# A hybrid conv / RG-LRU / mixture-of-experts step on one core: expert matmuls without high/low splits, the first chunk's matmuls reordered, token ranks dealt over gather rows

## The reference, cut to what matters

```python
def layer(x, cond, h0, on_grid, p):
    mod = (jax.nn.silu(cond) @ p['w_ada'] + p['b_ada'])[:, None, :]
    sh1, sc1, g1, sh2, sc2, g2 = jnp.split(mod, 6, axis=-1)
    h = rmsnorm(x, p['g_norm1']) * (1 + sc1) + sh1
    mix, h_last = token_mixer(h, h0, on_grid, p)     # u = h @ w_in (1024 x 7168), gates, two scans, w_o
    x = x + g1 * mix
    h = rmsnorm(x, p['g_norm2']) * (1 + sc2) + sh2
    return x + g2 * hier_moe(h, p), h_last

def hier_moe(h, p):
    ...   # group by argmax of 4 logits, then the top 2 of that group's 8 experts, weights in gates
    y = jnp.zeros_like(t)
    for e in range(N_EXPERTS):                        # 32; w1, w3: 1024 x 512, w2: 512 x 1024
        z = jax.nn.silu(t @ p['w1'][e]) * (t @ p['w3'][e])
        y = y + gates[:, e:e + 1] * (z @ p['w2'][e])
    return y.reshape(bsz, n, d)
```

## Time and profile before

| | |
|---|---|
| median of 3 runs | 1034.56 us (1031.83 to 1035.78) |
| the profiled execution | 1033.22 us |
| its span | 1031.5 us |
| PE busy (matmuls) | 937.8 us, 91% |
| DVE, ACT, POOL busy | 700.5, 569.7, 285.0 us |
| DMA packets | 69162, 294.97 MB, mean 286 GB/s |
| chain that ended last | PE 75%, DVE 13%, ACT 4%, DMA 2% |

### The profile page before, as it was taken

How to read it: one execution, slowest core, us unless ns; L and a number is a source line. 1 busy time by engine, 2 the same in 40 slices (tenths; PEclk the granted TensorE clock), 3 DMA queues, 4 the chain that set the end, 5 groups by cost and what they waited for, 6 DMA issues and landing times.

```text
span 1031.5 us, 12627 instructions
## 1 busy us (share of the span) xinstructions
PE 937.8 (91%) x4226; PEld 684.4 (66%) x4226; DVE 700.5 (68%) x881; ACT 569.7 (55%) x791; POOL 285.0 (28%) x214
## 2 busy tenths in 40 slices
PE   4499899998999999994899999999999999999980
PEld 2289797888999999444655656656656656566540
DVE  2389696859104442456788888887887888888835
ACT  4366536472334431311777677777767776776723
POOL 0235263635455553301011112112111211121010
PEclk9699899999999999995899999999999999999995
DMA  9992263646462656247589999999999999999804
GB/s 346 304 352 89 82 236 104 232 164 244 165 236 91 223 153 238 102 144 268 180 347 418 410 405 411 409 401 410 402 412 413 400 418 404 411 422 416 370 24 184
DMA packets 69162, 294.97 MB, mean 286 GB/s; under 512 B 8548, under 2 KB 19076, under 8 KB 56836
## 3 DMA queue, kind: packets, MB, share of 16 engines
q1 hardware_dynamic: 62740, 284.40, 71.5%
q0 software_dynamic: 5120, 6.31, 1.9%
q10 hardware_dynamic: 1264, 3.76, 1.0%
HBM read 290.20 MB, written 14.72 MB: 296 GB/s over the span
## 4 chain that ended last, share of the span: by engine, by line
PE 75%; DVE 13%; ACT 4%; issue 3%; SPq 3%; DMA 2%; POOL 0%; POOLq 0%; DVEq 0%; ACTq 0%
PE bank L936 21%; PE bank L919 13%; PE bank L920 12%; PE bank L796 7%; PE bank L798 6%; PE bank L797 6%; PE bank L845 3%; PE bank L909 2%; SPq L520 2%; DVE xcy L1504 2%; DVE lru L1558 1%; SPq L553 1%; ACT lru L1123 1%; DVE cp L1587 1%; DVE cp L1584 1%
## 5 line engine op out<-in xcount | busy, mean ns | idle before, releaser
L457 POOL TENSOR_TENSOR subs<-ring,subs 128x1024 fp32r<-128x1024 f32 x72 | 183.9, 2561 | 217.6 <-ACT subs L1046 217.6
L936 PE MATMUL bank<-ring,zT_buf 128*128 128x512 f32 x496 | 219.2, 595 | 0.0
L796 PE MATMUL bank<-h_hl,subs 128*128 128x384 f32 x512 | 177.7, 347 | 23.3 <-DVE h_hl L1482 14.7
L797 PE MATMUL bank<-h_hl,subs 128*128 128x384 f32 x512 | 175.0, 342 | 0.0
L798 PE MATMUL bank<-h_hl,subs 128*128 128x384 f32 x512 | 174.7, 341 | 0.0
L919 PE MATMUL bank<-subs,x_stack 128*128 128x512 f32 x384 | 162.5, 423 | 3.0 <-ACT x_stack L1310 1.7
L936 PEld LDWEIGHTS bank<-ring,zT_buf 128*128 128x128 f32 x496 | 91.9, 190 | 103.9 <-issue 103.8
L920 PE MATMUL bank<-subs,x_stack 128*128 128x512 f32 x384 | 154.1, 401 | 0.0
L513 DVE TENSOR_TENSOR subs<-ring,subs 128x1024 fp32r<-128x1024 f32 x96 | 112.2, 1222 | 25.5 <-ACT subs L1294 25.5
L796 PEld LDWEIGHTS bank<-h_hl,subs 128*128 128x128 f32 x512 | 98.0, 191 | 32.2 <-issue 18.2
L1046 ACT ACTIVATE subs<-ring 128x1024 fp32r<-128x1024 f32 x72 | 75.8, 1059 | 74.0 <-PE bank L798 66.6
(11 more groups left out here) (220 smaller groups left out, 1461.0 us busy)
## 6 DMA issues: line engine op xcount, KB each, us to landing
ring<-in_w SPq DMA_DIRECT2D x64, 2048.0 KB, 12.4
slot<-in_w SPq DMA_DIRECT2D x16, 2048.0 KB, 16.8
gate_w<-in_w SPq DMA_DIRECT2D x16, 2048.0 KB, 17.1
ring<-in_w_in SPq DMA_DIRECT2D x14, 2048.0 KB, 8.1
ring<-in_w_ada SPq DMA_DIRECT2D x12, 2048.0 KB, 20.0
ring<-in_w_rnn_out SPq DMA_DIRECT2D x2, 2048.0 KB, 7.8
ring<-in_w_conv_out SPq DMA_DIRECT2D x2, 2048.0 KB
ring<-in_w_o SPq DMA_DIRECT2D x2, 2048.0 KB, 7.9
```

Source lines behind the costliest of these rows:

```text
L457: eng.tensor_tensor(pair[:, 1], src, pair[:, 0].bitcast(F32), ALU.subtract).then_inc(done, 1)
L796: eng.matmul(ps[:, 0:T], pair[:, 1, k, :], x[:, 0, k, :], start=(k == 0), stop=False)
L797: eng.matmul(ps[:, 0:T], pair[:, 0, k, :], x[:, 1, k, :], start=False, stop=False)
L936: mm = eng.matmul(bank[4 + half][:, :], zT_buf[:, j * HALF:j * HALF + P], w[:, j, half * 512:(half + 1) * 512], start=(j == 0), stop=(j == ...
```

## The change

**Experts without splits.** w1 and w3 are multiplied as they are, in fp32. The transposed rows go into `x_T`, 64 columns wide, ACT copies one half of it and DVE the other. The product with w1 goes to the upper 64 partitions of a bank and the one with w3 to the lower 64, alternately (`hidden`). w2's two column halves are paired in the same way (`z_times`). No stage of high and low parts is left in an expert: ACT does one copy, the silu, the copy of the transposed z and one half of y; DVE one copy, one multiplication and the other half of y. The z product now stands in its own expert, not behind the next one's. The loops are unrolled by 8 experts.

**Slots.** `slot6` and `slot7` lie where the split buffers were; with them there are eight slots, and the loads of the first three experts' matrices are put before the first expert as far as the slots reach.

**The start.** The first three quarters of the first chunk are split by ACT between the blocks of h, and their low parts are made by DVE behind h rather than by POOL. PE takes three tiles together and goes through h block by block with the high parts of the weights; the low parts come last (`first_project`). The router's loads move from before chunk 4 to before chunk 12. In `START` two entries change places.

**Ranks.** The rank's one-hot is written in another order: rank 16a + b goes to row 4b + a of the list.

**Four matmuls of constants** (`ones` by `iota`) stand on PE between the token list and the first gathered rows.

```diff
-             ("adaR", 3), ("adaC", 2), ("adaC", 3)]
+             ("adaC", 2), ("adaR", 3), ("adaC", 3)]
...
-                if n == SLOTS:
+                if n == 12:
                     rows_of(wr[:, :, 0:NG], w_router_group[0].rearrange("(p k) n -> p k n", p=P), router_in)
...
+            def first_project(kind, x):
+
+                tiles = [open_tile((kind, m)) for m in range(SUBS)]
+                pairs = [quarter(quarter_of(kind, m))[1] for m in range(SUBS)]
+                for k in range(KD):
+                    eng.wait_ge(h_ready, k + 1)
+                    for m in range(SUBS):
+                        if k == 0:
+                            eng.wait_ge(hi_ready, m + 1)
+                        eng.matmul(tiles[m][:, 0:T], pairs[m][:, 0, k, :], x[:, 1, k, :], start=(k == 0), stop=False)
+                        eng.matmul(tiles[m][:, 0:T], pairs[m][:, 0, k, :], x[:, 0, k, :], start=False, stop=False)
+                for m in range(SUBS):
+                    wait_split(eng, m)
+                    for k in range(KD):
+                        mm = eng.matmul(tiles[m][:, 0:T], pairs[m][:, 1, k, :], x[:, 0, k, :],
+                                        start=False, stop=(k == KD - 1))
+                    mm.then_inc(tile_done, 1)
+                project(kind, 0, x, range(SUBS, CT))
...
+            def hidden(i, s, e, first):
+
+                eng.wait_ge(xT_a, e + 1)
+                eng.wait_ge(xT_v, e + 1)
+                if not first:
+                    eng.wait_ge(z_ready, e - 1)
+                wait_weights(eng, i, s, 0)
+                wait_weights(eng, i, s, 1)
...
+                for k in range(KD):
+                    eng.matmul(ps[HALF:P, :], x_T[:, k, :], w1_k[:, k, :], start=(k == 0), stop=(k == KD - 1))
+                    mm = eng.matmul(ps[0:HALF, :], x_T[:, k, :], w3_k[:, k, :], start=(k == 0), stop=(k == KD - 1))
+                mm.then_inc(h13_done, 1)
...
+                for j in range(JF):
+                    eng.matmul(ps[0:HALF, :], zT_buf[:, j * HALF:(j + 1) * HALF], w[:, j, 0:CW],
+                               start=(j == 0), stop=(j == JF - 1))
+                    mm = eng.matmul(ps[HALF:P, :], zT_buf[:, j * HALF:(j + 1) * HALF], w[:, j, CW:D],
+                                    start=(j == 0), stop=(j == JF - 1))
+                mm.then_inc(y_done, 1)
...
+                hidden(i, s, e, first)
                 if not last:
-                    transpose_rows(e + 1, 1 - s, 16 * (i + s + 1))
+                    transpose_rows(e + 1, 1 - s % 2, 16 * (i * (LAP // 2) + (s + 1) // 2 + 1))
                 transpose_z(e)
+                z_times(i, s, e, first)
...
+            for _ in range(4):
+                eng.matmul(bank[7][:, 0:T], ones[:, :], iota[:, :], start=True, stop=True)
...
+            def load_expert(e, s):
+
+                multiplied_in(e - 3)
+                load(e, s, 0)
+                multiplied_out(e - 3)
+                load(e, s, 1)
+                multiplied_in(e - 2)
+                load(e, s, 2)
...
-            feed(SUBS - 1)
+            feed(0)
             for k in range(KD):
                 eng.wait_ge(h_whole, k + 1)
                 eng.activation(h_hl[:, 0, k, :], xTr[:, k, :], ACT.Copy).then_inc(act_hi, 1)
+                if k < SUBS - 1:
+                    feed(k + 1)
...
+            for q in range(SUBS):
+                write_lo(eng, q, first_lo)
...
-                    last = eng.tensor_scalar(rank_oh[:, t, k, :], iota[:, 0:CAP], rank[:, t, k:k + 1],
-                                             None, ALU.is_equal)
+                    last = eng.tensor_scalar(rank_oh[:, t, k, :].rearrange("p (b a) -> p b a", a=CAP // 16),
+                                             iota[:, 0:CAP].rearrange("p (a b) -> p b a", b=16),
+                                             rank[:, t, k:k + 1], None, ALU.is_equal)
```

More of the change, by code:

```diff
@@ L449, in wait_split @@
         def wait_split(eng, q):
[L451 removed]
+            if q < SUBS:
+                eng.wait_ge(first_lo, q + 1)
+            else:
+                eng.wait_ge(lo_p, q - SUBS + 1)
         def write_lo(eng, q, done):
@@ L621, in _ @@
+            for s in range(3, LAP):
+                load_expert(s, s)
+            with eng.Fori(1, NE // LAP) as i:
+                for s in range(LAP):
+                    load_expert(i * LAP + s, s)
             eng.wait_ge(flag_ready, 1)
@@ new lines, in expert @@
+            def expert(i, s, last=False):
+                e = i * LAP + s
+                eng.wait_ge(h13_done, e + 1)
+                if not (isinstance(i, int) and i == 0 and s == 0):
+                    eng.wait_ge(z_ready, e)
+                eng.activation(sil, bank[2 + s % 2][HALF:P, :], ACT.Silu).then_inc(silu_done, 1)
+                if not last:
+                    rows_copy(e + 1)
+                zT_copy(e)
+                y_half(i, s, e)
+            rows_copy(0)
+            for s in range(LAP):
+                expert(0, s)
@@ L1365, in _ @@
+            with eng.Fori(1, NE // LAP - 1) as i:
+                for s in range(LAP):
+                    expert(i, s)
+            for s in range(LAP):
+                expert(NE // LAP - 1, s, last=(s == LAP - 1))
             eng.wait_ge(flag_ready, 1)
```

335 lines of the change are left out of this document (108 added, 227 removed).

## The result

The changed kernel takes 1010.08 us (median of 4 runs, 1008.69 to 1011.33) against 1035.13 us before, a ratio of 0.976 (95% interval 0.974 to 0.979). Predicted were 978.0, with a range of 960 to 1003: the sign was right, the gain is 25 us where the prediction had 55.

A forecast was written before the change was run, and what follows sets the result against it. PE bound the kernel before, loads the changed one. 494.9 + 2.8 + 450.6 lands the last load at 948.3; PE ends at 956.6, plus 29.5 less 9.5 plus 1.7 gives 978; range 960 to 1003.

The forecast's parts named there:

- First release at 485.4: Expert stage: the first expert's products with w1 and w3 end and free slots at 494.9 us, less 9.5 from the start.
- 88 loads of 5.12 us: Expert stage: loads are the bound; the 88 left after the first release take 5.12 us each, 450.6 in all.
- Dealing ranks 4 rows apart then evens it out, to 15.4: Expert loads: list order spreads rows over all queues, so the last queue needs 15.4 us an expert, not 16.2.
- From the last w3 to PE's end 13.4: End of the expert stage: after the last w3 lands at 943.2, PE needs 13.4 us, to 956.6.
- Tail 29.5: After the last w2 product: 29.5 us to the span's end, unchanged from before.
- Rival 1: Expert loads: queues stay uneven, 16.2 us an expert, 5.4 a load, +25 us, 1003 in all; chance 0.12.
- PE's 13.4 us: PE in one expert: 6.91 for w1 and w3, 2.94 open chain, 3.46 for w2, 0.1; bounds 13.0 and 14.4.
- The tiling drain: PE in an expert: four tiling-mode changes, no drain seen; at 0.16 us each 14.0 us an expert, the sum unchanged.
- rival 2: PE in the expert stage: clock falls in each expert, 16.4 us an expert, PE the bound, 1034.5 in all; chance 0.05.
- Constants: Before the first expert: four matmuls, 2.6 us or 5.2 at half clock, keep PE's clock full; without it 7 us more.
- The start, 9.5: Kernel start: first tile 8 us and fourth tile 10 to 11 us earlier; 9.5 us gained, bounds 4 and 12.
- a dense PE, which passes the gain on: Stage behind the start: PE is busy without waits, so the start's gain is passed on, 9.5 us.

The follow-up runs named there:

- e9: The changed kernel with ranks 0 to 15 on every second list row instead of every fourth: 998.81 us, ratio 0.966.
- e13: The changed kernel with the loads of expert 2's w1 and w3 held back until the first expert's products with w1 and w3 are done: 1019.68 us.
- e4: The kernel before with the change of the start alone put in: 1027.48 us, against 1033.58 for the kernel before.
- e15: The changed kernel with only an eighth of each w2 loaded from expert 3 on: 950.95 us, ratio 0.921.

## Why the prediction was wrong

Its sum, held against the profiled execution (span 1009.6, forecast 976.6):

1. *First release at 485.4* (494.9 less the start's 9.5): SP issues it at 491.9, 6.5 late. Of this 5.8 is the start: the list of rows is ready at 478.2 for a forecast 472.5. Some 2 us belong to this execution: in the 15 other traces of kernels with this start the first row transposes begin at 480.0 to 482.5 us, here at 483.5.
2. *88 loads of 5.12 us.* They took 25.6 us longer, 5.41 each. This is the step that failed: "Dealing ranks 4 rows apart then evens it out, to 15.4". It has two errors of nearly the same size. The deal did the reverse: the slowest queues need 16.3 where the mean is 15.85, 88 x 0.45 / 3 = 13 us, of which e9 took back 11. And 422 GB/s, one window's rate, was taken for all of the stage with even queues; with them it is 413 (e9, 600 to 900 us), and rows cost about twice their own packets. That is the other 12.
3. *From the last w3 to PE's end 13.4*: 965.79 to 979.24, 13.45. Right.
4. *Tail 29.5*: 30.3. Ranks in order or by two have 29.3 to 29.7, so this too is the deal.

6.5 + 25.6 + 0.1 + 0.8 is the 33 us missing. Rival 1 gave 1003 with "the order of ranks doesn't reach them, or a queue is late for another reason"; its outcome came about (16.34 us an expert, and a DMA releases PE), though by a third way: the order reaches the queues and makes them uneven. With 2.9 us from the start in place of 9.5 it makes 1009.6. It got 0.12 since the inferred cause looked well supported by 1.2 against 1.3 us. That agreement was of one number with one number, and the 1.3 counted as unevenness what rows cost every queue: in the table the queues of before lie 0.4 apart, 15.8 to 16.2.

The other steps. PE's 13.4 us: right (13.3 unheld). Halves overlap: right. The tiling drain: small. The first row transpose starts 0.53 us after the last pair of records where pairs are 0.43 apart, and the second 0.12 us after the first where the others are 0.07 apart: 0.15 us at this change of form, of which the kernel before shows nothing at the same place. It is within the 13.3, and whether it is the drain isn't shown. The clock (rival 2): real, absorbed. ACT, DVE and POOL hidden: right. SP's two new loads hidden: right, e13 puts their worth at 10 us. Constants: 5.3 us long, about as bounded (5.2), worth 2.5 to 3 and not 7.

The start, 9.5: its head was nearly right, what follows was not. The first chunk's landing near 36 was right (ACT splits it from 35.5). The modulation's last chunk was as late as before and its matmuls ran at 1.2 GHz in the profiled execution (3.64 us for 1.92), so that DVE began with h 2.2 us later than before; the first copy came at 51.2 for 48.5 to 49. Even so the first gate products were 9.3 us early, for a forecast 10 to 11. The step that failed is "a dense PE, which passes the gain on": PE waited for POOL's splits near 78 and 88 us (2.1 us lost), then for DVE at 153 us, and worked at the lower clock behind that (4.1 lost). In the trace of the start alone (e4) the same places take 10.2 us down to 8.1 and to 5.0. The kernel's time shows 6.1.

## What to carry to other kernels

Where a kernel is about to be bound by its loads, first measure them without the small transfers beside them: 3% of the bytes cost 8% of the time here. Rows of an indirect transfer that are skipped cost little, but where the used ones stand in the list changes how even the queues are (4 us worse and 7 us better than in order here); look at the spread of a load's 16 raises before and after a new order, and try a second order before believing a rule. A gain at the start of a program has to be followed to the stage where it counts: of 9.3 us at the first gate products 3.7 were left at 184 us. A stage that is bound by one resource hides the falls of another's clock, so a clock below 1 is no finding until that resource waits for nothing.

## What was not expected of the hardware

- Weights alone load at 428 GB/s with all 16 queues in step, 14.7 us an expert; moved rows cost about twice their packets' time, since weight packets become longer beside a gather (2.44 us a MB for 2.35), though not beside a scatter (2.45 with gathers alone). A skipped one costs next to nothing: 4 us for 3,968.
- Two products in the two column halves of the array start 0.01 us apart and together take 0.86 us, as long as a single one of 128 columns (0.864).
- With nothing to hold PE (e15) its clock fell 7 times in 31 experts with waits of 1.06 and 0.47 us around four transposes, and each fall cost 1.6 us.
